# High products first within a weight unit of a fused diffusion backbone kernel

## Chip, cores and metric

The kernel runs on one core of a Trainium2 chip. The metric is the device time of one execution in microseconds (us), the median of several.

## What is computed

Two layers of a diffusion backbone over 256 latent tokens of 2048 features, all in float32. Layer 0 mixes with attention (windowed and global heads, with 256 context tokens as further keys), layer 1 with a Hyena long convolution; each is followed by a squared-ReLU MLP. Cut to what matters here:

```python
h_lat = modulate(rms_norm(x, norm_mix_g[i]), sh1, sc1)
qa, qb, ka, kb, va, vb = split(h_lat @ attn_w_in)            # 2048 x 3072
y = attention(...) @ attn_w_out                              # 2048 x 2048
u = centred_short_conv(h_lat @ hy_w_in + b_in, ...)          # 2048 x 6144
y = hyena(...) @ hy_w_out + hy_b_out                         # 2048 x 2048
x = x + g1 * y
x = x + g2 * (square(relu(modulate(rms_norm(x, g), sh2, sc2) @ mlp_w1[i])) @ mlp_w2[i])   # 2048 x 8192 and back
```

Beside these there are the modulation vectors, `silu(c) @ mod_w`, whose weights are 2048 x 12288 a layer.

## The kernel before

Activations lie feature-major: `x` is [128, 16, 256], 16 blocks of 128 features by 256 tokens. Every float32 product is made of parts in the `F32R` type. An activation tile (`lat` or `alt`) is [128, 16, 512]: its columns 0 to 255 hold the rounded value (the high half), 256 to 511 what is left (the low half). A weight is split in the same way into `w_hi` and `w_lo`. The high half of a weight is multiplied with all 512 columns (line 358, the **high product**), the low half with the 256 high columns only (line 360, the **low product**), both added up in the same PSUM bank; a readout adds columns 256 to 511 to columns 0 to 255.

**Units.** Weights come in units of 512 rows by 256 columns ([128, 4, 256], 512 KB). Four units give 256 output features (a group, `g`), and an iteration `T` is 8 units, 512 output features. 90 iterations make 720 units: 4 for the queries, 2 for keys and values, 4 for the attention's output, 32 for MLP 0, 12 for Hyena's input, 4 for its output, 32 for MLP 1. A unit has 8 pairs of a high and a low product (4 row blocks `kk` by 2 column blocks `fb`); the 16 units for keys and values have 16, since they are applied to the context tile too.

**One unit's way.** Each of `raw`, `w_hi` and `w_lo` is a ring of 4 slots.

- SP (`sp_iter`, line 313) waits for `split_ready` of the unit 4 before and issues the transfer into `raw`. It issues the slabs of `mod_w` in the same queue.
- ScalarE (`act_split`, line 382) waits for the landing and for `units_done` of the unit 4 before, rounds `raw` into `w_hi` (line 386) and signals `hi_ready`.
- VectorE (`dve_split`, line 388) waits for `hi_ready`, subtracts, writes `w_lo` (line 390) and signals `split_ready`.
- TensorE (`pe_iter`, line 334) waits for `split_ready`, for the activation (`ready`: `norm_ready`, `hidden_ready`, `z_ready` or `head_ready`) and, at the first unit of a group, for `psum_free`; then it issues its pairs in the order high, low, high, low, and signals `units_done` with the last.

**What else is in the queues.** `act_iter` (line 565) and `dve_iter` (line 595) are written out for the 8 units of an iteration. VectorE's list around a unit: in the first iteration of a normalised stage `dve_normalise` (line 701) before each of the first four splits and `dve_norm_lo` (line 722, which writes the low half of `lat` and signals `norm_ready`) behind it; the readout of the last iteration at units 0, 3, 4 and 7 (`dve_head`, `dve_tail`); `dve_finish` (line 405) at unit 3, or ahead of unit 0 where a stage ends with it; the slabs of the modulation (line 402) at units 4 to 7. `pe_finish` (line 370) transposes the slabs' sums with 8 or 16 products (line 377) at the end of a stage. Ahead of keys and values TensorE waits also for `mod_ready` behind its `pe_finish`, which VectorE's reduction (line 409) and addition (line 414) serve. In the Hyena stage (`hyena`, line 1554) each of four rounds `c` has three iterations and the convolution (lines 1100, 1109 and 1119 on TensorE); the round's last VectorE work is line 1627, and then comes the next round's split. Line 989 is a set of column sums in the attention stage.

Of the kernel before, what the change touches and what calls it, by code (L numbers as in the profile page):

```python
# [25 lines left out]
P = 128  # L26
D = 2048
TOK = 256
KB = D // P
# [19 lines left out]
UNIT_KB = 4  # L49
UNIT_COLS = 256  # L50
SLAB = 1024
RING = 4
# [72 lines left out]
def build(nc, a):  # L125
# [3 lines left out]
    def sem(name):  # L129
        return stack.enter_context(nc.semaphore(name))  # L130

    def sb(name, shape, dt=F32, scope=None):
        return (scope or stack).enter_context(nc.sbuf_tensor(name, shape, dt))

    with stack:
# [20 lines left out]
        w_hi = sb("w_hi", [P, RING, UNIT_KB, UNIT_COLS], F32R)  # L156
        w_lo = sb("w_lo", [P, RING, UNIT_KB, UNIT_COLS], F32R)
# [55 lines left out]
        ps = stack.enter_context(nc.psum_tensor("ps", [P, 8, 512], F32))  # L213
# [21 lines left out]
        hi_ready, split_ready = sem("hi_ready"), sem("split_ready")  # L235
# [98 lines left out]
        def pe_iter(e, T, tile, ready, ctx_tile=None, stats=None, before=None):  # L334

            for n in range(8):
                if before:
                    before(n)  # L340
                if stats is not None and n == 7:
                    pe_stats(e, *stats)
                g = n // 4
                e.wait_ge(split_ready, 8 * T + n + 1)
                if ready:

                    e.wait_ge(*ready(n % 4))
                if n % 4 == 0:

                    e.wait_ge(psum_free, 2 * T + g - 1)  # L350
                for kk in range(UNIT_KB):
                    kb = (n % 4) * UNIT_KB + kk
                    for fb in range(2):
                        cols = slice(fb * P, (fb + 1) * P)
                        for t, bank in ((tile, 2 * g + fb), (ctx_tile, 4 + 2 * g + fb)):
                            if t is None:
                                continue
                            e.matmul(ps[:, bank, :], w_hi[:, n % RING, kk, cols], t[:, kb, :],  # L358
                                     start=(kb == 0), stop=False)
                            mm = e.matmul(ps[:, bank, 0:TOK], w_lo[:, n % RING, kk, cols], t[:, kb, 0:TOK],  # L360
                                          start=False, stop=(kb == KB - 1))
                mm.then_inc(units_done, 1)

        def pe_call(e, T, n, tile, ready, k=None):

            pe_iter(e, T, tile, ready(0))
            with e.Fori(1, n) as i:
                pe_iter(e, T + i, tile, ready(i), None, None if k is None else (k, i - 1))
# [285 lines left out]
        def pe_stats(e, k, c):  # L654

            e.wait_ge(squares, 4 * k + c + 1)
            for kk in range(4):
                mm = e.matmul(ps_all[:, ds(6 * 512 + TOK * c, TOK)], ones[:], sq[:, 0, kk, :],  # L658
                              start=(kk == 0), stop=(kk == 3))
            mm.then_inc(square_sums, 1)  # L660
# [204 lines left out]
        def _(e):  # L865
# [82 lines left out]
            with e.Fori(0, 4) as i:  # L948
                pe_iter(e, T_Q + i, lat, lambda j: (norm_ready, 1 + j))
# [741 lines left out]
```

## Time and profile before

| | before |
|---|---|
| time, median of 3 runs | 2738.21 us (2731.86 to 2744.17) |
| the profiled execution | 2733.1 us, span 2731.3 us |
| TensorE busy, products | 2520.0 us (92%) |
| TensorE busy, weight loads | 2096.5 us (77%) |
| VectorE busy | 1995.2 us (73%) |
| ScalarE busy | 1121.6 us (41%) |
| moved by DMA | 608.8 MB, 223 GB/s |
| mean granted clock of TensorE | 0.964 |

A product is pipelined, and its recorded end is modelled: what a product costs is the distance between the starts of two. "PE" is TensorE's products, "PEld" its weight loads, "DVE" VectorE, "ACT" ScalarE, "SPq" the queue of SP. In brackets behind an instruction stands the idle time of its engine before it and what ended it. The granted clock is given as a share of 2.4 GHz.

### The profile page before, as it was taken

To read this page: it belongs to the slowest core of one execution; us is meant where nothing else is said; L and a number is where in the kernel's file an instruction comes from. 1 tells how busy PE (TensorE), PEld (TensorE's weight loads), DVE (VectorE), ACT (ScalarE), POOL (GpSimd) and SP (SyncE) were. 2 spreads that over 40 slices of the span, in tenths; PEclk is the share of its full clock that TensorE was granted. 3 is DMA by queue.
4 is the path that set the end of the run, shared out by engine and by line. 5 is a ranking of instruction groups with operands and counts; after the bars stand their busy time and mean duration, and the time that the engine had idled before them with its cause. 6 is when DMAs were issued, how large, how long until landed. Compare 5 with 4: busy or idle time off the path is not lost.

```text
span 2731.3 us, 41835 instructions
## 1 busy us (share of the span) xinstructions
PE 2520.0 (92%) x13492; PEld 2096.5 (77%) x13492; DVE 1995.2 (73%) x2373; ACT 1121.6 (41%) x1494; POOL 0.2 (0%) x4
## 2 busy tenths in 40 slices
PE   7879986797999999999989999998899999999996
PEld 2338883586788888888868787787778888888885
DVE  6788658777987877878768888877676565555655
ACT  2224215643444444444434334233344444444442
POOL 0000000000000000000000000000000000000000
PEclk9989998898999999999999999999999999999998
DMA  8858844484998888888858567575556666666662
GB/s 308 315 185 270 299 142 115 132 266 157 322 315 277 282 275 282 273 283 281 275 171 276 190 211 253 168 254 188 181 172 190 190 188 191 187 189 191 187 185 98
DMA packets 441695, 608.80 MB, mean 223 GB/s; under 512 B 18363, under 2 KB 387228, under 8 KB 439580
## 3 DMA queue, kind: packets, MB, share of 16 engines
q1 hardware_dynamic: 440188, 598.53, 66.8%
q10 hardware_dynamic: 1440, 9.44, 0.9%
q8 instruction: 34, 0.56, 0.1%
q14 instruction: 33, 0.27, 0.0%
HBM read 597.41 MB, written 10.49 MB: 223 GB/s over the span
## 4 chain that ended last, share of the span: by engine, by line
PE 81%; DVE 11%; issue 3%; DMA 2%; ACT 2%; DVEq 0%; SPq 0%; ACTq 0%
PE ps L358 47%; PE ps L360 24%; PE ps L1109 2%; DVE w_lo L390 2%; DMA raw<-in_mlp_w 1%; PE ps L658 1%; PE ps L1119 1%; PE ps L924 1%; DMA raw<-in_mod_w 1%; DVE acc L402 1%; DVE hm L710 1%; DVE hm L718 1%; PE ps L888 1%; DVE lat L724 1%; DVE sm L1503 1%
## 5 line engine op out<-in xcount | busy, mean ns | idle before, releaser
L390 DVE TENSOR_TENSOR w_lo<-raw,w_hi 128x1024 fp32r<-128x1024 f32 x720 | 878.0, 1223 | 528.3 <-ACT w_hi L386 525.3
L358 PE MATMUL ps<-lat,w_hi 128*128 128x512 f32 x3200 | 1143.8, 400 | 69.8 <-DVE lat L724 58.1
L386 ACT ACTIVATE w_hi<-raw 128x1024 fp32r<-128x1024 f32 x720 | 759.7, 1060 | 1055.4 <-PE ps L360 941.8
L358 PE MATMUL ps<-alt,w_hi 128*128 128x512 f32 x2688 | 953.5, 398 | 9.2 <-DVE mod L414 5.7
L360 PE MATMUL ps<-lat,w_lo 128*128 128x256 f32 x3200 | 901.4, 282 | 0.0
L358 PEld LDWEIGHTS ps<-lat,w_hi 128*128 128x128 f32 x3200 | 610.1, 191 | 216.3 <-issue 75.7
L360 PE MATMUL ps<-alt,w_lo 128*128 128x256 f32 x2688 | 752.3, 280 | 0.0
L360 PEld LDWEIGHTS ps<-lat,w_lo 128*128 128x128 f32 x3200 | 614.0, 192 | 0.2
L358 PEld LDWEIGHTS ps<-alt,w_hi 128*128 128x128 f32 x2688 | 506.7, 189 | 130.4 <-DVE mod L414 6.0
L360 PEld LDWEIGHTS ps<-alt,w_lo 128*128 128x128 f32 x2688 | 508.8, 189 | 0.3
L402 DVE SCALAR_TENSOR_TENSOR acc<-slab,silu,acc 128x1024 f32<-128x1024 f32 x300 | 381.4, 1279 | 5.3 <-DMA slab<-in_mod_w 1.8
L496 DVE SCALAR_TENSOR_TENSOR x<-ps,mod,x 128x256 f32 (+1 forms) x160 | 69.8, 477 | 36.5 <-ACT lo_sum L486 36.0
L486 ACT ACTIVATE lo_sum<-ps,mod 128x256 f32<-128x256 f32 x144 | 59.2, 462 | 33.1 <-PE ps L360 33.1
L1183 ACT ACTIVATE spec<-ps 128x512 f32<-128x512 f32 x32 | 19.0, 593 | 109.7 <-PE ps L924 109.7
L1109 PE MATMUL ps<-z_tok,fwd 128*128 128x256 f32 x256 | 58.7, 382 | 5.5 <-ACT z_tok L1297 5.5
L1021 PE MATMUL ps<-kt,q_rot 128*128 128x512 f32 (+1 forms) x64 | 38.9, 697 | 26.7 <-ACT sm L1251 18.5
L1119 PE MATMUL ps<-back,y_spec 128*128 128x256 f32 x256 | 57.6, 381 | 2.8 <-DVE y_spec L1576 2.8
L1109 PEld LDWEIGHTS ps<-z_tok,fwd 128*128 128x128 f32 x256 | 47.4, 190 | 13.6 <-ACT z_tok L1297 7.4
L501 DVE TENSOR_TENSOR x<-x,lo_sum 128x512 f32 (+1 forms) x80 | 55.4, 692 | 2.8
L1119 PEld LDWEIGHTS ps<-back,y_spec 128*128 128x128 f32 x256 | 48.0, 190 | 10.8 <-DVE y_spec L1576 4.4
L924 PE MATMUL ps<-taps,fwd 128*128 128x512 f32 x128 | 56.3, 592 | 0.0
L559 DVE SCALAR_TENSOR_TENSOR u<-sum_sb,vecs,u 128x255 f32<-128x255 f32 x96 | 42.2, 481 | 16.3 <-ACT u L548 13.5
(180 smaller groups left out, 1405.8 us busy)
## 6 DMA issues: line engine op xcount, KB each, us to landing
raw<-in_mlp_w SPq DMA_DIRECT2D x512, 512.0 KB, 3.8
slab<-in_mod_w SPq DMA_DIRECT2D x352, 512.0 KB, 5.9
raw<-in_hy_w_in SPq DMA_DIRECT2D x96, 512.0 KB, 5.7
raw<-in_attn_w_in SPq DMA_DIRECT2D x48, 512.0 KB, 5.8
raw<-in_mod_w SPq DMA_DIRECT2D x32, 512.0 KB, 7.7
raw<-in_attn_w_out SPq DMA_DIRECT2D x32, 512.0 KB, 5.3
raw<-in_hy_w_out SPq DMA_DIRECT2D x32, 512.0 KB, 6.0
spec_dram<-spec ACTq DMA_DIRECT2D x8, 1024.0 KB, 7.9
```

The costliest lines, as they stand in the source:

```text
L358: e.matmul(ps[:, bank, :], w_hi[:, n % RING, kk, cols], t[:, kb, :], start=(kb == 0), stop=False)
L360: mm = e.matmul(ps[:, bank, 0:TOK], w_lo[:, n % RING, kk, cols], t[:, kb, 0:TOK], start=False, stop=(kb == KB - 1))
L386: e.activation(w_hi[:, n % RING], raw[:, n % RING], ACT.Copy).then_inc(hi_ready, 1)
L390: e.tensor_tensor(w_lo[:, n % RING], raw[:, n % RING], w_hi[:, n % RING].bitcast(F32), ALU.subtract).then_inc(split_ready, 1)
L402: e.scalar_tensor_tensor(acc[:, ac], slab[:, slot], scale, acc[:, ac], ALU.mult, ALU.add).then_inc(slabs_used, 1)
L486: ins = e.activation(lo_sum[:, g, fb], ps[:, 2 * g + fb, TOK:2 * TOK], ACT.Identity, bias=bias, scale=mod[:, ds(self.gate + f, 1)])
L496: ins = e.scalar_tensor_tensor(xf, ps[:, 2 * g + fb:2 * g + fb + 1, 0:TOK], mod[:, ds(self.gate + f, 1)], xf, ALU.mult, ALU.add)
L501: e.tensor_tensor(xg, xg, lo_sum[:, g], ALU.add).then_inc(psum_free, 1)
L559: ins = e.scalar_tensor_tensor(to, fr, vec("conv_w", 6 * KB * side + self.col + 2 * g + fb), to, ALU.mult, ALU.add)
L924: mm = e.matmul(ps[:, 2 + f % 2, :], fwd0[:, kb, f * P:(f + 1) * P], taps[:, o, kb, :], start=(kb == 0), stop=(kb == 1))
L1109: mm = e.matmul(ps[:, 4 + 2 * hf + f // 2, (f % 2) * 256:(f % 2 + 1) * 256], fwd[:, kb, f * P:(f + 1) * P], z_tok[:, hf, kb, :], start=(kb ...
L1119: mm = e.matmul(ps[:, 2 * o + hf, fb * TOK:(fb + 1) * TOK], y_spec[:, hf, f, fb * P:(fb + 1) * P], back[:, f, :], start=(f == 0), stop=(f ...
```

## The change

Within a unit TensorE waits for `hi_ready` (and the activation, and the bank, as before), issues all high products, then waits for `split_ready` and issues all low products. The products and their operands are the same, each bank still gets its first high product with `start`, and `units_done` is signalled with the last low product. Nothing changes on the other engines or in the transfers.

```diff
--- before.py
+++ after.py
@@ -341,7 +341,7 @@
                 if stats is not None and n == 7:
                     pe_stats(e, *stats)
                 g = n // 4
-                e.wait_ge(split_ready, 8 * T + n + 1)
+                e.wait_ge(hi_ready, 8 * T + n + 1)
                 if ready:
 
                     e.wait_ge(*ready(n % 4))
@@ -351,14 +351,19 @@
                 for kk in range(UNIT_KB):
                     kb = (n % 4) * UNIT_KB + kk
                     for fb in range(2):
-                        cols = slice(fb * P, (fb + 1) * P)
                         for t, bank in ((tile, 2 * g + fb), (ctx_tile, 4 + 2 * g + fb)):
-                            if t is None:
-                                continue
-                            e.matmul(ps[:, bank, :], w_hi[:, n % RING, kk, cols], t[:, kb, :],
-                                     start=(kb == 0), stop=False)
-                            mm = e.matmul(ps[:, bank, 0:TOK], w_lo[:, n % RING, kk, cols], t[:, kb, 0:TOK],
-                                          start=False, stop=(kb == KB - 1))
+                            if t is not None:
+                                e.matmul(ps[:, bank, :], w_hi[:, n % RING, kk, fb * P:(fb + 1) * P], t[:, kb, :],
+                                         start=(kb == 0), stop=False)
+
+                e.wait_ge(split_ready, 8 * T + n + 1)
+                for kk in range(UNIT_KB):
+                    kb = (n % 4) * UNIT_KB + kk
+                    for fb in range(2):
+                        for t, bank in ((tile, 2 * g + fb), (ctx_tile, 4 + 2 * g + fb)):
+                            if t is not None:
+                                mm = e.matmul(ps[:, bank, 0:TOK], w_lo[:, n % RING, kk, fb * P:(fb + 1) * P],
+                                              t[:, kb, 0:TOK], start=False, stop=(kb == KB - 1))
                 mm.then_inc(units_done, 1)
 
         def pe_call(e, T, n, tile, ready, k=None):
```

## Rows read from the trace of the kernel before

**Rows 1.** The page of the profile: busy times, and the chain that ended last

```profile
PE 2520.0 (92%) x13492; PEld 2096.5 (77%) x13492; DVE 1995.2 (73%) x2373; ACT 1121.6 (41%) x1494; POOL 0.2 (0%) x4
...
PE ps L358 47%; PE ps L360 24%; PE ps L1109 2%; DVE w_lo L390 2%; DMA raw<-in_mlp_w 1%; PE ps L658 1%; PE ps L1119 1%; PE ps L924 1%; DMA raw<-in_mod_w 1%; DVE acc L402 1%; DVE hm L710 1%; DVE hm L718 1%; PE ps L888 1%; DVE lat L724 1%; DVE sm L1503 1%
```

**Rows 2.** Windows of line 358: stretch, its length, PE, PEld, PEclk, DMA share, GB/s

```profile
175.00:2731.00 2556.00, 2085.88 (x5888) 1116.76 (x5888) 0.96 0.67 218
2000.00:2300.00 300.00, 299.98 (x864) 162.16 (x864) 1.00 0.63 191
```

**Rows 3.** Timeline, 2099 to 2101 us: start, us, engine, line, operation

```profile
2099.21 0.28 PE L360 MATMUL ps<-alt,w_lo 128*128 128x256 f32 x1
2099.33 0.39 PE L358 MATMUL ps<-alt,w_hi 128*128 128x512 f32 x1
...
2099.53 1.06 ACT L386 ACTIVATE w_hi<-raw 128x1024 fp32r<-128x1024 f32 x1 [1.71 <-PE ps L360]
2099.56 0.27 PE L360 MATMUL ps<-alt,w_lo 128*128 128x256 f32 x1
2099.56 0.19 PEld L358 LDWEIGHTS ps<-alt,w_hi 128*128 128x128 f32 x1
...
2100.62 1.23 DVE L390 TENSOR_TENSOR w_lo<-raw,w_hi 128x1024 fp32r<-128x1024 f32 x1 [1.55 <-ACT w_hi L386]
```

**Rows 4.** Waits of TensorE over the span: us in total, times, longest

```profile
PE ps L358 <- DVE lat L724: 58.1, 12, 14.9
...
PE ps L358 <- DVE w_lo L390: 14.5, 10, 2.9
```

**Rows 5.** Timeline of a normalised stage's start, VectorE and TensorE, 675 to 677 us

```profile
675.76 1.23 DVE L724 TENSOR_TENSOR lat<-hm,lat 128x1024 fp32r<-128x1024 f32 x1
...
677.13 0.47 PE L358 MATMUL ps<-lat,w_hi 128*128 128x512 f32 x1 [1.11 <-DVE lat L724]
```

**Rows 6.** Timeline of the start of keys and values, 292 to 294 us

```profile
292.50 0.17 DVE L414 TENSOR_TENSOR mod<-mod_part,vecs 128x8 f32<-128x8 f32 x1
...
294.05 0.49 PE L358 MATMUL ps<-lat,w_hi 128*128 128x512 f32 x1 [2.85 <-DVE w_lo L390]
```

**Rows 7.** Waits in 1500 to 2000 us, then the timeline of Hyena's output projection

```profile
PE ps L358 <- DVE w_lo L390: 5.4, 4, 2.8
...
1862.84 2.93 ACT L386 ACTIVATE w_hi<-raw 128x1024 fp32r<-128x1024 f32 x3
...
1865.93 2.36 DVE L390 TENSOR_TENSOR w_lo<-raw,w_hi 128x1024 fp32r<-128x1024 f32 x2
...
1867.21 0.80 PE L358 MATMUL ps<-alt,w_hi 128*128 128x512 f32 x1 [2.78 <-DVE w_lo L390]
```

**Rows 8.** Timeline of TensorE behind another stage start, 1543 to 1544 us

```profile
1543.97 0.63 PE L358 MATMUL ps<-lat,w_hi 128*128 128x512 f32 x1
1544.39 0.41 PE L360 MATMUL ps<-lat,w_lo 128*128 128x256 f32 x1
1544.61 0.63 PE L358 MATMUL ps<-lat,w_hi 128*128 128x512 f32 x1
```

**Rows 9.** MLP 0: waits in 560 to 800 us, timeline at 696, window 700 to 720

```profile
PE ps L358 <- DVE w_lo L390: 6.2, 5, 1.8
...
695.56 1.06 ACT L386 ACTIVATE w_hi<-raw 128x1024 fp32r<-128x1024 f32 x1 [3.38 <-DMA raw<-in_mlp_w]
...
696.65 1.22 DVE L390 TENSOR_TENSOR w_lo<-raw,w_hi 128x1024 fp32r<-128x1024 f32 x1
...
698.00 0.49 PE L358 MATMUL ps<-lat,w_hi 128*128 128x512 f32 x1 [1.60 <-DVE w_lo L390]
...
700.00:720.00 20.00, 19.64 (x114) 16.92 (x113) 17.97 (x17) 6.85 (x9) 0.00 (x0) 1.00 1.03 367
```

**Rows 10.** Timeline of runs of one kind: plain f32 products, and loads with one column

```profile
1489.75 1.46 PE L1109 MATMUL ps<-z_tok,fwd 128*128 128x256 f32 x6
...
401.07 1.19 PEld L989 LDWEIGHTS ps<-ones,probs_t 128*128 128x128 f32 x10 [0.80 <-ACT probs_t L1218]
```

## Prediction

> **What bounds the kernel now.** I read the page's busy shares and chain first. TensorE is busy for 92% of the span, and 71% of the chain that ended last lies in the two lines that the change reorders [rows 1]. The reader is to see that no other engine can give much: time is won or lost in the spacing of the products or in TensorE's idle time.
>
> The spacing comes next. Line 358 issues 5888 high products, each followed by one low product. Between 2000 and 2300 us, where TensorE never idles and the granted clock is 1.00 (2.4 GHz), 864 such pairs take 300 us: 0.347 us a pair [rows 2]. So the 5888 pairs are about 2043 us, three quarters of the kernel. The timeline splits the pair: a high product starts, 0.23 us later the low one, 0.11 to 0.12 us later the next high one [rows 3]. I call these the high slot (0.232) and the low slot (0.115). A weight load starts within 0.01 us of the product ahead of it and runs beside it; its recorded 0.19 us is longer than the low slot, so a record's length is not the time for which the loader is blocked.
>
> Last come the waits. What the change aims at is the wait of a first product of a unit for w_lo: 14.5 us in 10 waits [rows 4]. The list charges a wait to its last releaser only. The larger entry, 58.1 us for lat (line 724), is the start of the four normalised stages.
>
> In steady state neither half is late. At 2099.53 ScalarE starts a w_hi, released by the end of a unit; VectorE starts its w_lo at 2100.62 and needs 1.23 us, so it is there at 2101.85. That slot of the ring is read three units later, 3 x 2.78 = 8.3 us after 2099.53, at about 2107.9 [rows 3]. The lead is 6 us, whichever semaphore is asked.
>
> **The change part by part.** *Removed: the wait for w_lo ahead of the high products.* Four kinds of places:
>
> - Normalised stages (four, units 0 to 3). VectorE subtracts w_lo, then writes the low part of lat, in this order in its own queue. At 675.76 w_lo is finished and line 724 begins, at 676.99 lat is there, and TensorE starts at 677.13 [rows 5]. The new order still waits for lat first, and w_lo is older. Gain 0.
> - Keys and values, one wait. The idle time before 294.05 is 2.85 us, but TensorE also waits for mod, written until 292.67 behind VectorE's reduction; w_hi had long been there. So only 294.05 - 292.75 = 1.3 us is freed [rows 6].
> - Hyena stages and the output projection behind them, four waits of 5.4 us in all, the longest 2.8 us at 1867.21 [rows 7]. There ScalarE had begun w_hi at 1862.84 and so had it by 1863.9, early enough for TensorE, which idled for 2.78 us up to 1867.21; VectorE reached w_lo only at 1865.93, behind the stage's reduction. At such a stage start the slots are 0.42 and 0.22 us, about twice those of rows 3: the clock's lower level, 1.2 GHz [rows 8]. So eight high products take 8 x 0.42 = 3.4 us, more than the 2.8 us for which w_lo is late. Gain 5.4 us, all of it.
> - First quarter of MLP 0, five waits of 6.2 us in all [rows 9]. At 695.56 ScalarE rounds a unit that has just landed, VectorE is in the readout and starts w_lo at 696.65, TensorE starts at 698.00: with the new order near 696.7. But the DMA share is 1.03 in this stretch: each such wait is a unit that landed late, and TensorE, ahead by 1.3 us, would stand at the next late unit instead. The gains don't add up: the longest wait (1.8 us) bounds what is carried out of the stretch, and the stage behind it begins with a wait for VectorE's alt, which may absorb that too. Bounds 0 and 2 us; I take 1.
>
> Sum of removed waits: 0 + 1.3 + 5.4 + 1 = 7.7 us; bounds 3 (the freed time is met again at a DMA or VectorE wait) and 11.
>
> *Added: a second wait in the middle of each of 720 units.* No wait in mid-unit exists today. The nearest row is the border of two units, which has two or three waits already: the low product at 2099.21 ends a unit (its end released ScalarE at 2099.53), the high one at 2099.33 follows at 0.12 us [rows 3]. A satisfied wait costs nothing visible there. Bounds: 0, and one low slot, 0.115 us, on each unit: 83 us. I take 0, since the border is the same case. Behind the waiting instruction there are only the low products; the high ones are already out. Nobody else waits for them but units_done, signalled at the unit's end as now. ScalarE, VectorE and SP's queue issue what they did; no DMA is moved. The cover of this zero is the 6 us lead; without it, a late w_lo is paid in the middle instead of at the start, never twice.
>
> *Moved: the order of 16 loads and 16 products of a unit (32 in the keys' units).* Now each high slot carries a low-half load and each low slot a high-half load. Afterwards 5168 of the high slots (5888 - 720) carry a high-half load and as many low slots a low-half load. All loads are 128 x 128 of the same type, 0.19 us either way. If a slot's length depends on its own product and on one load, all sums stay: 0.232 + 0.115. The trace speaks for that: per column the high slot is 0.232/512 = 0.453 ns, the low slot 0.115/256 = 0.449 ns, the same rate in both, which looks like the rate of the streaming and not like a charge for switching. On the lower clock the slots are 0.42 and 0.22 us, again 2 to 1 [rows 8].
>
> Bounds of the move. From below: plain f32 products, back to back and all alike, are x6 in 1.46 us, less the last one's 0.38, over 5: 0.216 us for 256 columns [rows 10]. Line 358's products in this form take 0.453 ns a column and these 0.84; half of that, 0.42 ns, would make a pair of 768 columns 0.324 us, 0.023 less than now. That is 5168 x 0.023 = 119 us of gain. From above: a load that can no longer hide behind 256 columns. Ten loads with a single column each follow one another at (1.19 - 0.19)/9 = 0.111 us [rows 10], under the low slot; the recorded 0.19 us as a slot would cost 5168 x 0.075 = 388 us. I take 0, as the 0.111 row is nearest to a run of loads.
>
> In the timeline a load for all 128 rows starts while the product ahead of it, on all 128 rows too, is still running [rows 3]. The Trainium skill ("TensorE: Matmul & The Clock Gate", Part 3, The mechanism) says that a load overlaps a running matmul only when the row groups differ. The trace does not agree, and the measurement decides; by that rule every load would stand exposed in both orders alike.
>
> **Total.** -7.7 + 0 + 0 = -7.7 us. The profiled execution took 2733.1 us (span 2731.3), 5.1 below the median of the three runs, 2738.2. Against its own time the sum gives 2725.4; against the median, 2730.5. I forecast 2730. About 0.5% (14 us) is what a measurement of this kernel can tell from no change.
>
> **Rivals.**
>
> *Alike products stream faster (faster).* If the 8% that a pair takes above the plain f32 rate is the price of alternating sizes, halves or of two products on one bank in a row, a uniform run loses it: 2730 - 119 = 2611. For: at the lower clock there is no excess (0.64 us a pair, twice 0.32), so something beside the array sets it. Against: equal cost per column in both slots. A part of it is enough: 1.2 ns a pair brings -14 us. The Trainium skill (the same page, Back-to-back issue gap) gives columns over 2.4 GHz plus about 2.5 ns. By it a pair would be 0.325 us in either order, and the trace, with 0.347, does not agree. Chance of a gain above 14 us in all, with the waits at their upper bound or saved low-clock time helping: 0.28.
>
> *Load-bound low run (slower).* Place: the 7 low-to-low slots of a unit. Today a low slot is followed by a high slot, in which a late load can catch up; in a run of low products there is none. If a low-half load beside a running product needs the 0.232 - 0.216 = 0.016 us by which the high slot exceeds the plain rate, the slot becomes 0.131 and, with the high slot unchanged, costs 5168 x 0.016 = 83 us: 2813. It decides from 0.119 us a slot (22 us to use up the gain and cross 0.5%). Against: 0.111 us with bare loads [rows 10]. The Trainium skill (the same page, LDWEIGHTS) gives the load as its columns over 1.2 GHz, 0.107 us; the trace agrees with its 0.111. Chance of over 0.5% slower, by this or by the mid-unit wait: 0.13.
>
> *The freed waits come back.* TensorE is merely early for the next transfer or VectorE chain, and nothing is left: 2736. It lies in the same band as the forecast; chance 0.17 beside 0.42 for the forecast itself.
>
> **How the numbers follow.** The forecast's own range is 2720 to 2742 (waits 3 to 11 us, run scatter of 6 us). Beyond it every nanosecond of spacing is 5.2 us. The 80% range takes in a spacing from 9 ns less (-47) to 6 ns more (+31): 2683 to 2761; the two ends of the rivals, 2611 and 2813, are left out with about a tenth each. Faster by over 0.5%: 0.28; within: 0.59; slower: 0.13.
>
> **What would show it.** Right: the profile after has slots of 0.232 between high products and 0.115 between low ones in 2000 to 2300 us, some 864 high products in these 300 us, the wait list without the 5.4 us in the hyena stages, lat's 58 us unchanged. Wrong: another count of products in the same 300 us (917 for the faster rival, 831 for a low slot of 0.131); a new entry for the wait for w_lo in mid-unit; or low-clock stretches that moved.

## The result and the profile after

The kernel after takes 2731.2 us, the median of 20 runs (2725.6 to 2736.5); the kernel before, in 20 runs taken beside them, 2743.0 us (2731.9 to 2757.8). The ratio is 0.9947 with a 95% interval of 0.9932 to 0.9962, so 0.5% faster, at the edge between two of the forecast's bands. The profiled execution took 2730.95 us (span 2729.2), only 2.1 us less in span than that of before. The two profiled executions differ less than the two medians, and that is the first thing to explain: the runs of before lie 26 us apart, those of after 11.

The busy times and the chain of the page after, beside [rows 1]:

```profile
PE 2526.8 (93%) x13492; PEld 2111.7 (77%) x13492; DVE 1995.0 (73%) x2373; ACT 1120.9 (41%) x1494; POOL 0.2 (0%) x4
...
PE ps L356 47%; PE ps L365 24%; PE ps L1114 2%; DVE w_lo L395 1%; PE ps L663 1%; PE ps L929 1%; DVE acc L407 1%; PE ps L893 1%; DMA raw<-in_mlp_w 1%; PE ps L1124 1%; DVE hm L715 1%; DVE hm L723 1%; DMA raw<-in_mod_w 1%; DVE lat L729 1%; DVE sm L1508 1%
```

Nothing has moved between the engines. TensorE's waits over the span, beside [rows 4]:

```profile
PE ps L356 <- DVE lat L729: 58.5, 12, 14.9
...
PE ps L356 <- DVE mod L419: 7.6, 2, 5.7
...
PE ps L356 <- ACT w_hi L391: 2.6, 3, 1.0
...
PE ps L356 <- DVE sum_sb L516: 2.4, 2, 1.2
...
PE ps L356 <- DVE alt L528: 1.9, 1, 1.9
```

The 14.5 us for w_lo are gone; lat's 58 us are where they were. The other four lines show what took over: mod at keys and values (1.9 us more than before's 5.7), and in MLP 0 the late w_hi and VectorE's readout. Hyena's output projection, beside [rows 7]:

```profile
1858.47 3.88 ACT L391 ACTIVATE w_hi<-raw 128x1024 fp32r<-128x1024 f32 x4
...
1859.04 1.09 PE L382 MATMUL ps<-const,acc 128*128 128x128 f32 x8 [3.42 <-DVE acc L407]
1860.17 1.23 DVE L414 TENSOR_REDUCE mod_part<-ps 128x8 f32<-128x1024 f32 x1
1860.29 1.98 PE L356 MATMUL ps<-alt,w_hi 128*128 128x512 f32 x4 [0.16 <-issue]
...
1861.64 1.23 DVE L395 TENSOR_TENSOR w_lo<-raw,w_hi 128x1024 fp32r<-128x1024 f32 x1
```

TensorE starts 0.16 us behind its transposes instead of 2.78, while VectorE is still reducing. In steady state the timeline of TensorE, beside [rows 3], has merged rows (start of the first, length of the run):

```profile
2102.29 1.12 PE L365 MATMUL ps<-alt,w_lo 128*128 128x256 f32 x8
2103.24 2.00 PE L356 MATMUL ps<-alt,w_hi 128*128 128x512 f32 x8
2105.09 1.12 PE L365 MATMUL ps<-alt,w_lo 128*128 128x256 f32 x8
```

Eight low products take 0.95 us and eight high ones 1.85: a unit is 2.80 us. Within the run of low ones the spacing is (1.12 - 0.28)/7 = 0.120 us. To compare spacings I count the high products in one stretch of MLP 1 without waits, 2120 to 2520 us (windows of the high products' line: stretch, length, PE, PEld, PEclk, DMA share, GB/s). Before, then after:

```profile
2120.00:2520.00 400.00, 400.00 (x1155) 216.38 (x1154) 1.00 0.62 189
```

```profile
2120.00:2520.00 400.00, 287.00 (x1147) 206.23 (x1148) 1.00 0.62 188
```

After does 8 products fewer, 0.7% slower in this stretch. From the starts of successive units the medians are 2.773 us before and 2.793 after. But before does not always run at 2.773. In MLP 0 its windows are

```profile
800.00:860.00 60.00, 60.00 (x171) 31.92 (x170) 1.00 0.89 295
880.00:950.00 70.00, 70.00 (x203) 37.77 (x202) 1.00 0.83 278
970.00:1040.00 70.00, 70.00 (x199) 37.24 (x199) 1.00 0.84 276
```

199 products in one 70 us and 203 in another, TensorE busy throughout at the full granted clock. MLP 0 is four quarters, each an up half and a down half of four iterations (32 units). By the medians of the unit starts the four down halves, Hyena's third round and its output projection ran at 2.830 us, all other stages at 2.773. After has 2.793 in every stage. So there were two theories to tell apart. **Two effects:** the removed waits, and a spacing that before takes at two values and after at one between them. **Rival:** the waits alone, with before's scatter from elsewhere.

### The profile page after: what moved, and what is told of

Read it like the earlier page. It is cut to its first block, busy times and chain, and to the rows that moved or that the text cites. A ratio compares the mean times of both kernels' runs of the same rounds, so it can differ in the third digit from the quotient of the medians.

```text
span 2729.2 us, 41835 instructions
## 1 busy us (share of the span) xinstructions
PE 2526.8 (93%) x13492; PEld 2111.7 (77%) x13492; DVE 1995.0 (73%) x2373; ACT 1120.9 (41%) x1494; POOL 0.2 (0%) x4
## 4 chain that ended last, share of the span: by engine, by line
PE 82%; DVE 11%; issue 3%; ACT 2%; DMA 2%; DVEq 0%; SPq 0%; ACTq 0%
PE ps L356 47%; PE ps L365 24%; PE ps L1114 2%; DVE w_lo L395 1%; PE ps L663 1%; PE ps L929 1%; DVE acc L407 1%; PE ps L893 1%; DMA raw<-in_mlp_w 1%; PE ps L1124 1%; DVE hm L715 1%; DVE hm L723 1%; DMA raw<-in_mod_w 1%; DVE lat L729 1%; DVE sm L1508 1%
## 5 line engine op out<-in xcount | busy, mean ns | idle before, releaser
L356 PE MATMUL ps<-lat,w_hi 128*128 128x512 f32 x3200 | 839.2, 399 | 65.6 <-DVE lat L729 58.5
L356 PEld LDWEIGHTS ps<-lat,w_hi 128*128 128x128 f32 x3200 | 587.3, 192 | 177.5 <-issue 49.7
L356 PE MATMUL ps<-alt,w_hi 128*128 128x512 f32 x2688 | 698.2, 395 | 7.8 <-DVE mod L419 5.7
L356 PEld LDWEIGHTS ps<-alt,w_hi 128*128 128x128 f32 x2688 | 488.1, 190 | 96.7 <-DVE mod L419 6.0
L365 PEld LDWEIGHTS ps<-lat,w_lo 128*128 128x128 f32 x3200 | 448.7, 192 | 32.0 <-DVE w_lo L395 0.4
L365 PE MATMUL ps<-lat,w_lo 128*128 128x256 f32 x3200 | 464.1, 284 | 0.0
L365 PEld LDWEIGHTS ps<-alt,w_lo 128*128 128x128 f32 x2688 | 374.7, 191 | 25.8
L365 PE MATMUL ps<-alt,w_lo 128*128 128x256 f32 x2688 | 389.1, 283 | 0.0
```

The costliest lines, as they stand in the source:

```text
L356: e.matmul(ps[:, bank, :], w_hi[:, n % RING, kk, fb * P:(fb + 1) * P], t[:, kb, :], start=(kb == 0), stop=False)
L365: mm = e.matmul(ps[:, bank, 0:TOK], w_lo[:, n % RING, kk, fb * P:(fb + 1) * P], t[:, kb, 0:TOK], start=False, stop=(kb == KB - 1))
```

## Experiments

**1. Before once more (before_again).** No edit.

> The kernel before, unchanged, profiled a second time. In the trace of before 536 units outside stalls run at 2.773 us and 184 (the down halves of MLP 0, Hyena round 2, Hyena's output) at 2.830 us; after, all run at 2.793. Theory A (the alternating order has two spacings, and which one a stage gets changes from execution to execution): time the same as before within 0.3%, but this trace has its 2.830 us stages in other places, and its own time is off 2733 by about 0.057 us for each further unit in the longer spacing. Theory B (the spacing belongs to the stage): the same 184 units, 2733 us within 2 us. Rival C (the scatter of before's 20 runs, 2732 to 2758, comes from the opening of 178 us or from transfers): unit times as in the first trace, and the time differs elsewhere.

Measured: ratio 0.9998 [0.9970, 1.0027], runs from 2731.6 to 2764.6. Its trace, the same three windows:

```profile
800.00:860.00 60.00, 60.00 (x174) 32.44 (x173) 1.00 0.88 298
880.00:950.00 70.00, 70.00 (x203) 37.76 (x202) 1.00 0.85 284
970.00:1040.00 70.00, 70.00 (x199) 37.21 (x198) 1.00 0.84 278
```

The first stretch now has 174 products instead of 171: the first down half of MLP 0 has changed to 2.773. The attention's output, the first up half of MLP 0 and two more Hyena rounds went the other way. The spacing is not a property of the stage, as theory A had it. Its arithmetic does not carry the time, though. Counted one by one, 143 units stand at 2.830 in the first trace and 159 here, since a stage need not keep one value to its end. The 16 more are 1 us, and this execution took 6.4 us more than the first; its first unit starts 9.3 us later, so the opening varies too.

The two spacings are two rhythms. At 2.773 the slots repeat after two pairs (in MLP 1: 0.231, 0.112, 0.233, 0.117 us, high and low in turn) or after one (0.230, 0.117). At 2.830 they repeat after three: 0.236, 0.113, 0.233, 0.117, 0.241, 0.120 (around 850 us in the first trace). In both traces every change from one spacing to the other falls where a wait or other products of TensorE stand between two units. A run of units that nothing interrupts keeps the rhythm that it has; all of MLP 1 up to its last iteration is such a run.

**2. The order alone (reorder_only).** The unit waits for both halves first, as before, and issues in blocks, as after.

```diff
-                e.wait_ge(hi_ready, 8 * T + n + 1)
+                e.wait_ge(split_ready, 8 * T + n + 1)
...
-                e.wait_ge(split_ready, 8 * T + n + 1)
                 for kk in range(UNIT_KB):
```

> The order of after, but the unit waits for split_ready ahead of its high products, as before. Theory A (two effects: waits -8 us, spacing to 2.793 everywhere): 8 us above after, about 2739 us, a ratio to before of about 0.998; TensorE's waits for w_lo are back at 14 us in some 10 waits; units 2.793 us in every stage. Theory B (the gain is the waits alone, the spacing nets out): ratio 1.000, 12 to 14 us above after. Rival C (the gain is the spacing alone): ratio 0.995, as after.

Measured: 2742.4 us, ratio 0.9978 [0.9955, 1.0001], runs of 2740.5 to 2749.3. Units are 2.793 us in every stage, and the wait is back:

```profile
PE ps L356 <- DVE w_lo L394: 13.5, 10, 2.9
```

This parts the gain, not sharply. From before to here (order alone) it is 0.2%, with an interval that just reaches none, so theory B is not excluded by the time. From here to after (waits alone) it is 9 to 11 us by the medians of the two measurements of after (2731.2 and 2733.6), which were not taken beside this kernel, and 6 to 8.5 us by the three ratios to before. Theory A's 2739 us was 3 us low. The traces part it better, stage by stage: from the first unit of Hyena to that of MLP 1 this kernel takes 552.7 us and after 543.6 (543.2 in its second trace). That is 9 us, for 5.0 us of removed waits. Where the rest comes from the windows of 20 us from the first transpose at a stage's start show, this kernel and then after (Hyena's rounds 2 to 4 and the output projection):

```profile
1546.63:1566.63 20.00, 13.44 (x48) 9.67 (x48) 0.84 0.84 283
1654.03:1674.03 20.00, 12.93 (x44) 9.39 (x45) 0.83 0.84 288
1762.26:1782.26 20.00, 13.64 (x48) 9.68 (x48) 0.85 0.84 280
1869.39:1889.39 20.00, 11.97 (x41) 8.53 (x42) 0.83 0.74 253
```

```profile
1542.39:1562.39 20.00, 14.10 (x52) 10.30 (x53) 0.91 0.85 287
1647.96:1667.96 20.00, 14.33 (x52) 10.44 (x53) 0.91 0.84 285
1753.52:1773.52 20.00, 14.37 (x52) 10.28 (x53) 0.91 0.85 285
1859.04:1879.04 20.00, 14.00 (x50) 10.03 (x51) 0.91 0.77 255
```

A mean granted clock of 0.83 is 20 x 0.17 x 2 = 6.8 us at the lower level, 0.91 is 3.6 us. By the trace's record of the clock each such stretch is 6.8 us in this kernel and 3.4 in after; some begin just ahead of the window. Over the four stretches there are 181 high products against 206: 25 at 0.349 us are 8.7 us. TensorE falls silent for 3.4 us ahead of the transposes in both; what is gone is the second idle stretch behind them (0.5, 1.3, 0.5 and 2.8 us). After's second trace and those of experiments 4 and 7, which have no such wait either, show 3.4 us at all four starts too.

The same sum for the order alone: 2.793 us throughout costs 720 x 0.020 = 14 us above 2.773, and the units at 2.830 cost before 8 us in the first trace and 9 in the second. So in the traced executions the order is a loss of 5 to 6 us; in MLP 1 alone this kernel takes 6.0 us more than before. A gain of 0.2% would need executions of before with more units at 2.830 than the traced two. The scatter speaks for them: the runs of the eight other kernels that were timed often spread over 9 to 17 us, those of before over 26 to 33. But no long execution of before was traced, so this stays argued.

**3. After once more (after_again).** No edit.

> The kernel after, unchanged, on the same chip as the three below. Theory A (block order has one spacing, alternating order two): units of 2.793 us in every stage again, its runs within 12 us of each other while those of before spread over 25 us or more, ratio near 0.995. Rival (the spacing of after varies too, and the first trace met one case of it): some stage with another unit time than 2.793.

Measured: 2733.6 us, ratio 0.9957 [0.9935, 0.9978], units of 2.793 us in all stages. The runs span 17 us (2727.3 to 2743.9), more than the 12 expected, against 29 for before on that chip. One spacing holds in both traces of after; where the scatter that is left lies was not traced.

**4. Blocks in one unit of eight (first_only).** Block order in unit 0 of an iteration, alternation in the others.

```diff
+                lag = len(pairs) if n == 0 else 0
+                for p in pairs[:lag]:
+                    high(*p)
+                e.wait_ge(split_ready, 8 * T + n + 1)
+                for k, p in enumerate(pairs):
+                    if lag + k < len(pairs):
+                        high(*pairs[lag + k])
+                    mm = low(*p)
```

> Block order (all high, wait, all low) in unit 0 of each iteration alone, alternating order with the wait ahead in the other seven. The waits that open a stage (one of keys and values, four around Hyena: 1.3 + 5.4 us) are all at unit 0, those of MLP 0 not. Theory A (waits and spacing are separate): stage-opening gains as after, Hyena rounds with 3 us of low clock each instead of 5 to 10, and the other units at 2.773 or 2.830 as before: 7 to 10 us below before, runs spread as before. Theory B (one block unit in eight also breaks the longer spacing): the other units at 2.773 in all stages, about 2720 us and a ratio near 0.991, below after.

Measured: 2749.1 us, ratio 1.0013 [0.9996, 1.0031]. Of the waits for w_lo ahead of a unit 4.8 us are left, 4.3 of them in MLP 0's first quarter, so the stage openings were gained as in after, and yet nothing is left of it:

```profile
2120.00:2520.00 400.00, 385.78 (x1136) 212.08 (x1135) 1.00 0.61 186
```

1136 products where before has 1155. By the medians the alternating units run at 2.830 in every stage but the first of MLP 0, where waits lie between them (2.869). Both theories fail: mixing the orders fixes the spacing, but at the longer value. The run shows that 2.830 can come with alternation in any stage, whatever its transfers and its VectorE work, and it shows what that spacing costs: MLP 1, all at 2.773 in both traces of before, does 1.6% less in the same time.

**5. Alternation with a lag (lag1, lag2).** The loop of experiment 4 with `lag = 1` and `lag = 2`.

> Alternating order, but the low product runs one pair behind: high 0, high 1, low 0, high 2, low 1, ... The mid-unit wait stands behind the first high product, so the waits for w_lo stay nearly as before (0.23 us less each). The low product no longer follows the high one of its own bank. Theory A (two spacings belong to every alternation of high and low): stages of 2.773 and of 2.830 us, time as before within 0.3%. Theory B (they come from two products in a row into one bank): one spacing, at or below 2.773, about 2737 us. Each stage in the longer spacing adds 1.8 us for 32 units.

> Alternating order with the low product two pairs behind: three high products ahead of the first low one, three low ones at the end of a unit, high and low of a pair of neighbours in the same bank as before. Theory A (any break in the alternation at the unit's border sets the spacing back, as the blocks do): one spacing, between 2.773 and 2.793 us, waits 0.5 us shorter each: about 2729 us. Theory B (two spacings belong to alternation, wherever it stands): 2.773 and 2.830 us stages, near before.

Measured: lag 1 gives 2752.3 us, ratio 1.0034 [1.0012, 1.0056], and 1136 products in the 400 us; lag 2 gives 2741.6 us, 1.0001 [0.9976, 1.0025], and 1142. Each has one spacing in nearly all stages, 2.820 and 2.806 us: theory A of lag 1 is wrong, and so is the bound of 2.793 in that of lag 2. Theory B of lag 1 is wrong too, since the single value is far above 2.773, and so is that of lag 2, which has one value and not two. Each pattern of issue has its own unit time; none so far is below 2.773. The slots of the longer rhythm (0.241, 0.236, 0.120) stand in the units of both lags too.

**6. Smaller blocks (twos, fours, twos_first).** Two high and two low in turn; four and four; and twos with a full block in unit 0. In the 16 units for keys and values the sizes are doubled. Twos was written as another loop with the same order.

```diff
+                size = 2          # twos; 4 in fours; len(pairs) if n == 0 else 2 in twos_first
+                for k in range(0, len(pairs), size):
+                    for p in pairs[k:k + size]:
+                        high(*p)
+                    if k == 0:
+                        e.wait_ge(split_ready, 8 * T + n + 1)
+                    for p in pairs[k:k + size]:
+                        mm = low(*p)
```

> Order high, high, low, low within each row block (two of each in turn), the mid-unit wait ahead of the first low product, so only two high products run ahead of w_lo. Theory A (the 20 ns a unit above 2.773 belong to each switch from low to high products): 4 switches a unit, 2.773 + 4 x 0.020 = 2.85 us a unit, 2731 + 720 x 0.060 = 2774 us. Theory B (they belong to the length of a run of low products, whose loads fall behind): 2.773 us a unit, about 2725 us with the waits of before mostly back. Theory C (two spacings as in the alternating order): a mixture of 2.773 and 2.830 us stages, near before.

> Four high, four low, twice a unit; mid-unit wait behind the first four. Theory A (block orders have one spacing, a little above 2.773 whatever the block): between the 2.787 of twos and the 2.793 of eights, one value in all stages, waits for w_lo gone where they are under 0.9 us: ratio to before 0.994. Theory B (each pattern has its own spacing with no order in it): another value, up to 2.82 as with one pair of lag; each 10 ns a unit is 7 us.

> Block order in unit 0 of each iteration, two high and two low in turn in the other seven. Alone, the second ran 2.787 us units, with 6 us of waits for w_lo left in mid-unit; unit 0 opens the stages in which most of them lie. Theory A (a spacing belongs to the order of one unit and stays when orders are mixed): 2.787 in seven units, 2.793 in unit 0, waits near zero outside MLP 0, about 2 to 4 us below the pure form: ratio to before 0.993 or less. Theory B (mixing orders can set a longer spacing, as it did for the alternating order, which ran 2.830 in all stages behind a block unit): units above 2.80, ratio above 0.995.

Measured: twos 2732.0 us, ratio 0.9939 [0.9920, 0.9958]; fours 2740.6, 0.9985 [0.9961, 1.0009]; twos_first 2725.5, 0.9945 [0.9924, 0.9966], before having 2741.1 on that chip. Windows of twos, fours and twos_first:

```profile
2120.00:2520.00 400.00, 360.65 (x1149) 174.86 (x1150) 1.00 0.61 189
```

```profile
2120.00:2520.00 400.00, 311.22 (x1142) 194.87 (x1141) 1.00 0.61 187
```

```profile
2120.00:2520.00 400.00, 351.37 (x1150) 178.73 (x1148) 1.00 0.61 188
```

Twos has 2.787 us a unit, fours 2.807, eights 2.793: the unit time does not follow the number of switches (4, 2, 1), so all theories on a price per switch fall. Twos removes a good part of the waits, though only two products run ahead of w_lo; TensorE still waits for it in mid-unit, where before waited 14.5 us:

```profile
PE ps L363 <- DVE w_lo L393: 5.9, 9, 1.4
```

Twos_first brings these down to 2.4 us, at 2.787 in nearly every stage, and it has the lowest median and the shortest trace of the study (span 2719.6), but its ratio cannot be told from that of after. No version here is shown to beat after.

**7. One bank after another (one_bank).** Block order with the loops over column blocks and row blocks exchanged.

```diff
-                pairs = [(kk, fb, t, bank) for kk in range(UNIT_KB) for fb in range(2)
+                pairs = [(kk, fb, t, bank) for fb in range(2) for kk in range(UNIT_KB)
```

> Block order, but all four row blocks of one column block after one another, so that up to four products in a row add into one bank, where after changes the bank with each product. Theory A (the bank plays no part in the spacing): 2.793 us units, time within 5 us of after. Theory B (alternating banks saves something, which the block order gains over the pair on one bank before): longer units in all stages; the pair's excess of 0.023 us over the plain f32 rate would grow.

Measured: 2734.5 us, 1146 products in the 400 us (after: 1147), units of 2.793 us, and within a unit the same slots to 2 ns. In block order the bank plays no part.

**8. Short low products (low128, low128_alt).** The block order and the alternating one, with half the columns of the low product left out.

```diff
-                                mm = e.matmul(ps[:, bank, 0:TOK], w_lo[:, n % RING, kk, fb * P:(fb + 1) * P],
-                                              t[:, kb, 0:TOK], start=False, stop=(kb == KB - 1))
+                                mm = e.matmul(ps[:, bank, 0:P], w_lo[:, n % RING, kk, fb * P:(fb + 1) * P],
+                                              t[:, kb, 0:P], start=False, stop=(kb == KB - 1))
```

> The order of after, low products on the first 128 of the 256 high columns only (a part of the low half of the product is left out). It measures what a weight load takes beside a short product. Theory A (a low slot of 0.120 us is set by the load): the low slots stay near 0.111 to 0.120 us, units near 2.79 us, time within 10 us of after. Theory B (each product pays its columns and a fixed 13 ns, load hidden): low slots 0.067 us, units near 2.37 us, TensorE waits for transfers in many stages, since 736 units would need their 512 KB in less time than now.

> The order of before with the low products on 128 of the 256 high columns (a part of the low half of the product is left out). In block order this gave low slots of 0.111 us, bound by the load, and a unit of 2.747. In alternation a late load has the high slot to catch up. Theory A (a load needs its 0.111 us and one load fits behind each product, wherever it stands): the next high product still waits for its load, started with the low product: low slot 0.11, unit about 8 x (0.231 + 0.112) = 2.74 us. Theory B (loads run ahead by more than one): low slot 0.067 us, unit near 2.4 us and TensorE waiting for transfers.

Measured: 2703.9 us in blocks, 2687.9 in alternation, one run each. In blocks the slots are as theory A had them, but the time is 27 us below after, where it allowed 10: the unit is 2.747 us, 46 ns shorter. The run of low products is

```profile
2102.36 1.00 PE L365 MATMUL ps<-alt,w_lo 128*128 128x128 f32 x8
2103.21 2.07 PE L356 MATMUL ps<-alt,w_hi 128*128 128x512 f32 x8
```

By the starts, seven of its slots are 0.110 to 0.114 us, with 128 columns; with 256 they were 0.120. Half the work saves 8 ns of a slot: a low slot in blocks is within 8 ns of what a load takes. In alternation:

```profile
2099.91 0.22 PE L360 MATMUL ps<-alt,w_lo 128*128 128x128 f32 x1
2099.97 0.44 PE L358 MATMUL ps<-alt,w_hi 128*128 128x512 f32 x1
2100.25 0.22 PE L360 MATMUL ps<-alt,w_lo 128*128 128x128 f32 x1
2100.31 0.44 PE L358 MATMUL ps<-alt,w_hi 128*128 128x512 f32 x1
```

The low slot is recorded as 0.06 us and the high one as 0.28, so the start times agree with theory B; but the pair is 0.34 us, against 0.347 with the full low product, and the unit 2.720, so the time is near theory A's 2.74. The reading that fits both is that a high product recorded early still waits for its load; in blocks, too, the first high slot behind a low run is 0.283 us and the next 0.233. By this reading, which no run tests by itself, a recorded start is not the start of the streaming when a load is late, and 0.232 and 0.115 in before need not be the true shares of the two products; only the pair's sum is sure.

## Why the prediction was right, and where not

**Forecast 2730, measured 2731.** The forecast time came from 2738.2 less 7.7 us. In 20 runs before has 2743.0, so the gain is 12 us by medians and 14.5 us by the ratio, nearly twice the sum. That the time was met to 1 us is luck: the three runs of before that I had were low ones by 5 us, and the gain was too small by about as much.

**Waits: mechanism right, mis-sized (7.7 us predicted, some 10 by the traces, 6 to 8.5 by the ratios of the runs).**
- Normalised stages: 0 predicted. Lat's wait is 58.5 us against 58.1 [rows 4]. Right.
- Keys and values: 1.3 us predicted. TensorE's idle time there fell from 2.85 us [rows 6] to 1.9, up to mod. Right within 0.4 us.
- MLP 0: 1 us predicted, 0 to 2 as bounds. From the first unit of MLP 0 through its first quarter reorder_only needs 197.9 us and after 197.4. The ahead TensorE stands at the next unit that landed late, as argued (w_hi 2.6 us in 3 waits, after).
- Hyena and its output: 5.4 us predicted, 9 measured (experiment 2). This is the mis-sized term: I counted the idle time alone. It is followed by time at the lower clock, and that was halved from 6.8 to 3.4 us at each of the four starts. The prediction named low-clock time only as a chance for the faster band, and low-clock stretches that moved as a sign that it was wrong. They did: in the trace of before the four are 6.8, 3.4, 6.8 and 10.2 us.

**Mid-unit wait: 0 predicted.** Reorder_only, without it, and after, with it, have the same unit time, 2.793 us, and 1148 and 1147 products in 400 us. Right.

**Moved loads and products: 0 predicted; the step's reason was wrong.** That a column costs the same in both slots, 0.453 and 0.449 ns, rested on recorded starts. In the later part of a run of one kind the slots are 0.227 and 0.120 us by the starts (0.443 and 0.469 ns a column), not proportional, and experiment 8 shows that the low slot is nearly the load's. Their sum is again 0.347, which is why 0 came out nearly right for one spacing, with 862 products in 2000 to 2300 us against 864. The first slots of a run are longer, though (0.233 and 0.236): after pays 20 ns a unit above 2.773, 14 us over 720 units.

What the prediction missed altogether is the second spacing of before, 2.830. It was to be seen in the trace that its rows came from: 199 against 203 products in two windows of MLP 0. I had read the spacing in MLP 1 alone [rows 2]. At 57 ns a unit it would add up to 41 us if all units had it. The order alone changes the time by 0.2% (interval 0 to 0.45%). That it gains this by trading the mixture for 2.793 fits the scatter of the runs but is not shown; in the two traced executions of before the trade loses 5 to 6 us (experiment 2).

**The rivals.** *Alike products stream faster:* did not happen. High slots late in a run fell from 0.232 to 0.227, low ones rose. The Trainium skill ("TensorE: Matmul & The Clock Gate", Back-to-back issue gap) gives for an isolated product the columns over 2.4 GHz plus about 2.5 ns, and an estimate from it is 0.216 and 0.109 us; the trace does not agree. The 8% that this rival puts on a pair above the plain rate is 7% by its own numbers (0.347 against 0.324). *Load-bound low run:* it happened in kind, at a price of 3 to 5 ns a slot instead of 16. The low slot rose to 0.120 us, just past the 0.119 from which I had let this rival decide, but that threshold took the high slot as unchanged, and it fell. Loads with a single column each followed at 0.111 us [rows 10], low products of 128 columns at 0.112. The Trainium skill (the same page, LDWEIGHTS) gives a load as its columns over 1.2 GHz, an estimate of 0.107 us for 128; the trace agrees within 5 ns. *The freed waits come back:* only in MLP 0.

**The bands.** The ratio of 0.9947 lies in the faster band by 0.03% and its interval reaches into the other. The 0.28 and 0.59 that I gave them were fair for a sum of 7.7 us and too low on the faster side for a gain of 12 to 14.5.

**Left open.** Why the alternating order has two spacings and what picks one, and why each pattern has its own (2.787, 2.793, 2.806, 2.807, 2.820), was not settled. For the block order banks are excluded (experiment 7); for the alternating order they were only changed together with the pattern (lag 1). The stage with its own transfers and VectorE work is excluded as the sole cause (experiments 1 and 4); how products, loads and other engines' accesses stand in time to one another when a stage begins was not tried.

## What to carry to other kernels

Measure the spacing of a product stream by counting products in windows of several stages, and in two executions, before giving a reorder a cost of zero: here one order had two spacings 2% apart, up to 41 us over the kernel, against some 10 us for the waits in question. A wait that opens a stage can cost its idle time and also a longer stretch at the lower clock: read the granted clock behind it. Waiting for the first half of an operand only pays where TensorE is truly at the wait; in a stretch bound by transfers the time comes back at the next late unit.

## What the hardware showed unexpectedly

- The same instructions in the same order ran at 2.773 or 2.830 us a unit, in rhythms of one or two and of three pairs, at full granted clock with TensorE never idle, and changed between them only where something stood between two units; three block sizes and two lags kept one value each in nearly all stages.
- A block unit once in eight put nearly all other units at 2.830 (first_only), while a block unit ahead of twos left them at 2.787 (twos_first).
- Leaving out a sixth of the columns of each pair (128 of 768) saved 7 ns of 347 in alternation. The pair of 0.340 us that is left is about one high slot late in a run (0.227) and one load (0.112).
- A removed idle stretch of 0.5 to 2.8 us, parted by eight transposes from one of 3.4 us, took 3.4 us of lower clock with it at each of four stage starts.
